# Reordering the triangular inverses of a two-block transformer kernel: one half of the heads a step ahead in the first level, two starts moved to levels four and five, and one wait on VectorE dropped

## The chip, the cores and the metric

The kernel runs on one core of one Trainium2 chip. The metric is the device time of one execution in microseconds (us). Three runs of the kernel before gave 1217.25, 1214.26 and 1218.85 us; their median is 1217.25 us.

The engines are named as in the profile: PE is the matrix engine (TensorE), PEld its weight loads, DVE the vector engine, ACT the scalar engine, POOL GpSimd, and SP the engine that issues the loads of the weights.

## What is computed

The reference runs two blocks on 256 tokens of width 1024. The first has two kinds of attention, cross attention to a memory, and a feed-forward part. The second has one layer with a recurrence over the tokens (RWKV-7) and one with latent attention, each with a feed-forward part. All of it is in 32 bits. The change lies in the recurrence, of which this is the core:

```python
def step(state, inp):
    r_t, w_t, k_t, v_t, a_t, b_t = inp
    sa = jnp.einsum('bhvk,bhk->bhv', state, a_t)
    state = (state * w_t[:, :, None, :] + sa[..., None] * b_t[:, :, None, :]
             + v_t[..., None] * k_t[:, :, None, :])
    return state, jnp.einsum('bhvk,bhk->bhv', state, r_t)
...
y = rwkv7_scan(rh, heads(decay, RWKV_HEADS), kh, vh, -kk, kk * lrh)
y = head_group_norm(y, a_lnx_g[i], a_lnx_b[i])
y = y + jnp.sum(rh * kh * a_r_k[i], axis=-1, keepdims=True) * vh
```

There are 12 heads of 64 channels. The sum over `rh * kh * a_r_k` in the last line, one number for each head and token, is what the change calls the head sums.

## The kernel before, in words

**The large products.** Most of the time goes to products of activations with weights. Weights come from HBM in units of 1 MB into a ring of four (`sync_program`). ACT makes a rounded part `w_hi` of each unit (line 2169), DVE the rest `w_lo` (line 1405, or in quarters on line 1413), and PE multiplies in three passes (line 650, the helper through which nearly all matmuls go). During the recurrence PE uses none of the streamed weights; the ring is full and the loads stand still.

**The recurrence in chunks.** The 256 tokens are cut into four chunks of 64. In a chunk the step by step update becomes products of 64x64 blocks, and needs for each head the inverse of a 64x64 triangular matrix. The 48 inverses (4 chunks of 12 heads) are computed in four batches: batch n holds the chunks 2*(n // 2) and 2*(n // 2) + 1, one on either half of the partitions, and the six heads from 6 * (n % 2) on. Batches 0 and 1 come first, then 2 and 3. The even batches use the buffers of side q = 0 (`step_142`, `inverse_140`, PSUM banks 0 and 1), the odd ones those of q = 1 (`step_143`, `inverse_141`, banks 2 and 3).

**From the products to the first inverse.** For two heads at a time PE makes the chunk products (16 instructions for the two heads in the trace, `a_and_r` and `b_and_k`) into four PSUM banks that go around. DVE masks each head's bank into SBUF (`masked`, line 2037), and PE waits for the head four places back before it writes a bank again. `first_inverse` (lines 2051 and 2054) builds the inverse to the first order, `1 + A`, for a batch, and `turn` (line 2059) transposes it. The head sums are three matmuls of 512 columns into banks 0 to 2 (`r_k` and `same_head`), before the products of heads 6 and 7; ACT copies them out (line 2569), and PE waits for these copies before it writes banks 0 to 3 for the inverses. DVE waits for the three matmuls too, in `first_inverse(0)` on line 2046.

**The levels.** Five levels double the size of the blocks that are inverted. In a level, each batch goes through a chain between two engines: "first" on PE (the chunk products times the inverse so far, 24 instructions in the trace), "first" on DVE (the mask, line 2078, tile `step`), "second" on PE (24 instructions), and "second" on DVE (the addition to `inverse_t`, line 2084, then `turn`). The `turn` feeds the "first" of the next level. After the fifth level of batch n, `turn(n + 2)` starts batch n + 2 in the same buffers, and needs `first_inverse(n + 2)`.

**The order.** `recurrence_order` gives a list of pieces, and PE, DVE and ACT each run the pieces of this one list that concern them, in its order; an engine never runs ahead of the piece that it waits for. In between lie pieces of other work: "rows" (the centred values, matmuls with `centring`), "keys" (transposes of the keys, line 1294), "high" and "low" (the parts of the next weights on ACT and DVE), "rest" (on DVE, lines 2093 and 2098), and behind the fifth level the solution itself ("rhs", "u", "state", "y"). The list of before begins so:

```python
    for level in range(1, LEVELS + 1):
        order += [("first", 0, level), ("first", 1, level)]
        order += [("rows", 2 * level - 4, 0)] if 2 <= level < 4 else []
        order += [("high", level - 1, 0)] if level <= 4 else []
        order += [("keys", level - 2, 0)] if 2 <= level < NC + 1 else [("batch", 2, 0)] if level == 1 else []
        order += [("second", 0, level), ("second", 1, level)]
        order += [("rows", 2 * level - 3, 0)] if 2 <= level < 4 else []
        order += [("batch", 3, 0)] if level == 1 else [("rest", level - 2, 0)] if level < 4 else []
```

"batch" is `first_inverse` and concerns DVE alone. Ahead of the list DVE masks the heads, makes and turns the first inverses of batches 0 and 1, and then does four operations of a token shift (`shift_pair(5, ...)`, line 1925), which the first "rows" needs.

Of the kernel before, what the change touches and what calls it, by code (L numbers as in the profile page):

```python
# [11 lines left out]
ALU = mybir.AluOpType  # L12
# [19 lines left out]
C = 64  # L32
NC = S // C
LEVELS = 5
# [571 lines left out]
def recurrence_order():  # L606


    order = []
    for level in range(1, LEVELS + 1):  # L610
        order += [("first", 0, level), ("first", 1, level)]
        order += [("rows", 2 * level - 4, 0)] if 2 <= level < 4 else []
        order += [("high", level - 1, 0)] if level <= 4 else []
        order += [("keys", level - 2, 0)] if 2 <= level < NC + 1 else [("batch", 2, 0)] if level == 1 else []
        order += [("second", 0, level), ("second", 1, level)]
        order += [("rows", 2 * level - 3, 0)] if 2 <= level < 4 else []
        order += [("batch", 3, 0)] if level == 1 else [("rest", level - 2, 0)] if level < 4 else []
# [546 lines left out]
def recurrence_tensor(k, matmul, heads_turned, attention, way_part, projection):  # L1164
    nc, PE, bank, ident = k.nc, k.nc.tensor, k.bank, k.ident[:, :]
# [70 lines left out]
    for h in range(0, RW_HEADS, 2):  # L1236
        if h in (0, 6):
            PE.wait_ge(*k.dve_once.at("r", h // 6))
        if h == 6:
            PE.wait_ge(*k.dve_once.at("rk", 0))  # L1240
            PE.wait_ge(*k.raw_made.all("ain"))
            for n in range(3):
                matmul(bank[n][:, :].rearrange("p (k t) -> p k t", k=2), k.same_head[:, :], k.rk[:, 2 * n:2 * n + 2, :], True,
                       True).then_inc(k.pe_once.sem, 1)
# [12 lines left out]
    for piece, n, level in recurrence_order():  # L1257
        if piece == "first":
            q, m, h0 = n % 2, n // 2, 6 * (n % 2)
            at = LEVELS * m + level - 1  # L1260
# [639 lines left out]
def recurrence_vector(k, attention, product, low_part, split):  # L1900
# [131 lines left out]
    def side_columns(n):  # L2032
        return k.masks[:, n:n + 1, :].to_broadcast((P, 6, C))
# [7 lines left out]
    def first_inverse(n):  # L2041
# [3 lines left out]
        if n == 0:  # L2045
            V.wait_ge(*k.pe_once.all("rk"))
# [14 lines left out]

    V.wait_ge(*k.dve_once.all("r"))
    for half in range(2):
        for h in range(6 * half, 6 * half + 6):
            masked(h)
        first_inverse(half)
        V.wait_ge(*k.xt0.at("batch", half))
        turn(half)
    shift_pair(5, 0)
    shift_pair(5, 1)  # L2070
    rest = k.rest
    for piece, n, level in recurrence_order():
        if piece == "batch":
            first_inverse(n)
        elif piece == "first":
            q, at = n % 2, LEVELS * (n // 2) + level - 1
            V.wait_ge(*k.w_p.at(f"q{q}", at))
            V.tensor_tensor(k.w[q][:, :, :], bank[2 * q][:, 0:6 * C].rearrange("p (h t) -> p h t", h=6), side_columns(2 + level),
                            ALU.mult).then_inc(k.w_v.of(f"q{q}"), 1)
# [832 lines left out]
```

## Time and profile before

| what | value |
|---|---|
| median of three runs | 1217.25 us |
| the profiled execution, its own time | 1218.09 us |
| its span in the trace | 1216.8 us |
| granted TensorE clock, mean | 0.975 |
| PE busy | 1167.8 us (96%) |
| PEld busy | 1107.5 us (91%) |
| DVE busy | 755.1 us (62%) |
| ACT busy | 572.2 us (47%) |
| POOL busy | 68.0 us (6%) |

Every time of the trace is counted from the start of the span. The profiled execution's own time is 1.3 us above its span, and 0.84 us above the median. PEclk is the share of full speed that the throttle granted to PE: 1.00 is 2.4 GHz, 0.50 is 1.2 GHz. The recurrence with its inverses lies between 588 and 686 us; the five levels of batches 0 and 1 end at 632.9 us.

### The profile page before, as it was taken

What the parts mean: (1) busy time and instruction counts of PE and PEld (TensorE: products, weight loads), DVE (VectorE), ACT (ScalarE), POOL (GpSimd) and SP (SyncE); (2) the same over time, 40 slices, a digit from 0 to 9 for tenths busy, and PEclk for the clock granted to TensorE, in tenths of its full rate; (3) what the DMA queues carried; (4) which work ended last, traced back from release to release, by engine and by line L of the source; (5) the groups of instructions that cost most, each with busy time, mean ns of one, the idle gap of its engine ahead of it and who ended that gap; (6) DMA issues with size and microseconds to landing.
All of it is one profiled execution on the core that took longest, in us unless ns stands there. A gap on an engine that the chain in (4) does not pass through costs nothing.

```text
span 1216.8 us, 22608 instructions
## 1 busy us (share of the span) xinstructions
PE 1167.8 (96%) x9917; PEld 1107.5 (91%) x9917; DVE 755.1 (62%) x982; ACT 572.2 (47%) x761; POOL 68.0 (6%) x137
## 2 busy tenths in 40 slices
PE   7998999999999999899799999999999999999998
PEld 7897978879999999889688999999987779999998
DVE  4565766556565556757786676555576776655553
ACT  5445555245444334574342545434365664543443
POOL 2310020100000000300000000000001000000000
PEclk9997999999999999998899999999999999999999
DMA  7941343424555555522000355554544205545551
GB/s 257 335 167 69 139 173 140 173 104 144 186 191 176 194 185 177 197 104 107 33 3 3 98 191 177 181 200 174 186 163 170 105 4 194 184 175 194 187 176 67
DMA packets 30237, 185.03 MB, mean 152 GB/s; under 512 B 3579, under 2 KB 6848, under 8 KB 9148
## 3 DMA queue, kind: packets, MB, share of 16 engines
q1 hardware_dynamic: 24464, 174.07, 40.0%
q0 software_dynamic: 2464, 7.11, 1.9%
q10 hardware_dynamic: 3212, 2.42, 0.6%
q8 instruction: 78, 1.28, 0.4%
q14 instruction: 19, 0.16, 0.0%
HBM read 180.18 MB, written 3.41 MB: 151 GB/s over the span
## 4 chain that ended last, share of the span: by engine, by line
PE 83%; DVE 7%; ACT 5%; issue 2%; DMA 2%; POOL 0%; SPq 0%; ACTq 0%; DVEq 0%
PE bank L650 80%; ACT w_hi L2169 2%; DMA w_raw<-in_weights 2%; DVE w_lo L1405 1%; PE bank L829 1%; ACT exps L2270 1%; DVE stats L1596 1%; PE bank L664 1%; DVE inverse_rms_rows L1531 1%; DVE logits L1588 1%; ACT x_channels_hi L2231 1%; DVE inverse L2059 0%; DVE mem_channels_gained L1440 0%; DVE inverse_t L2084 0%; ACT mem_squares L2175 0%
## 5 line engine op out<-in xcount | busy, mean ns | idle before, releaser
L1405 DVE TENSOR_TENSOR w_lo<-w_raw,w_hi 128x2048 fp32r<-128x2048 f32 x160 | 364.6, 2291 | 217.5 <-ACT w_hi L2169 217.3
L2169 ACT ACTIVATE w_hi<-w_raw 128x2048 fp32r<-128x2048 f32 x164 | 311.9, 1913 | 115.8 <-DMA w_raw<-in_weights 110.2
L650 PE MATMUL bank<-x_channels_hi,w_hi 128*128 128x256 f32 x1424 | 234.3, 288 | 10.5 <-DVE w_lo L1405 4.2
L650 PE MATMUL bank<-x_channels_lo,w_hi 128*128 128x256 f32 x1424 | 230.4, 285 | 0.0
L650 PE MATMUL bank<-x_channels_hi,w_lo 128*128 128x256 f32 x1424 | 222.8, 280 | 0.0
L650 PEld LDWEIGHTS bank<-x_channels_hi,w_hi 128*128 128x128 f32 x1424 | 198.8, 194 | 15.5 <-issue 6.9
L650 PEld LDWEIGHTS bank<-x_channels_lo,w_hi 128*128 128x128 f32 x1424 | 196.3, 192 | 0.0
L650 PEld LDWEIGHTS bank<-x_channels_hi,w_lo 128*128 128x128 f32 x1424 | 193.4, 191 | 0.0
L650 PE MATMUL bank<-hidden_hi,w_lo 128*128 128x256 f32 x528 | 103.4, 284 | 0.0
L650 PE MATMUL bank<-hidden_hi,w_hi 128*128 128x256 f32 x528 | 102.0, 280 | 0.0
L650 PE MATMUL bank<-hidden_lo,w_hi 128*128 128x256 f32 x528 | 101.7, 279 | 0.0
L650 PEld LDWEIGHTS bank<-hidden_lo,w_hi 128*128 128x128 f32 x528 | 79.8, 188 | 0.0
L650 PEld LDWEIGHTS bank<-hidden_hi,w_hi 128*128 128x128 f32 x528 | 79.3, 188 | 0.5 <-issue 0.5
L650 PEld LDWEIGHTS bank<-hidden_hi,w_lo 128*128 128x128 f32 x528 | 79.5, 188 | 0.0
L2415 ACT ACTIVATE gates<-gates 128x512 f32<-128x512 f32 x33 | 20.9, 633 | 91.2 <-DVE gates L1762 91.1
L2419 ACT ACTIVATE hidden_hi<-values 128x512 fp32r<-128x512 f32 x33 | 20.9, 632 | 89.2 <-DVE values L1769 89.2
L2270 ACT ACTIVATE exps<-logits,stats 128x128 f32<-128x128 f32 (+1 forms) x56 | 25.1, 448 | 52.6 <-DVE stats L1596 52.1
L1764 DVE TENSOR_TENSOR values<-bank,inverse_rms_rows 128x512 f32<-128x512 f32 x33 | 22.8, 690 | 37.9 <-PE bank L650 37.9
L1771 DVE TENSOR_TENSOR hidden_lo<-values,hidden_hi 128x512 fp32r<-128x512 f32 x33 | 22.9, 693 | 23.1 <-ACT hidden_hi L2419 23.1
L2231 ACT ACTIVATE x_channels_hi<-x,gain_columns 128x256 fp32r<-128x256 f32 x40 | 17.6, 501 | 38.0 <-DVE x L1503 38.0
L1762 DVE TENSOR_TENSOR gates<-bank,inverse_rms_rows 128x512 f32<-128x512 f32 x33 | 22.6, 685 | 20.7 <-ACT inverse_rms_rows L2250 20.7
L2666 POOL TENSOR_SCALAR channel_inverse_rms<-channel_mean_squares 128x2 f32<-128x2 f32 x5 | 1.2, 232 | 569.4 <-DVE channel_mean_squares L1537 569.4
(429 smaller groups left out, 1608.4 us busy)
## 6 DMA issues: line engine op xcount, KB each, us to landing
w_raw<-in_weights SPq DMA_DIRECT2D x164, 1024.0 KB, 4.8
bias_rows<-bias_lines POOLq DMA_DIRECT2D x3, 768.0 KB, 4.7
mem_rows<-in_mem POOLq DMA_DIRECT2D x2, 1024.0 KB, 5.6
bias<-bias_rows ACTq DMA_DIRECT2D x1, 1536.0 KB, 13.7
xn<-in_x SPq DMA_DIRECT2D x1, 1024.0 KB, 4.9
out<-xn SPq DMA_DIRECT2D x4, 256.0 KB, 2.2
wide_masks<-in_triangle_masks POOLq DMA_DIRECT2D x1, 832.0 KB, 6.8
bias<-bias_rows ACTq DMA_DIRECT2D x1, 768.0 KB, 5.0
```

What stands on the lines that cost most here:

```text
L650: return nc.tensor.matmul(out, lhs, rhs, start=start, stop=stop)
L664: t = nc.tensor.transpose(b[:, j * P:(j + 1) * P], k.turn_source(stage, tok, k0 + j), ident)
L829: m = nc.tensor.transpose(b[:, c:c + P], e[:, c:c + P], ident)
L1405: V.tensor_tensor(k.w_lo[:, s, :], k.w_raw[:, s, :], k.w_hi[:, s, :].bitcast(F32), ALU.subtract).then_inc(k.lo_done, 1)
L1762: V.tensor_tensor(k.gates[:, par, :, :], pairs(2 * par), R, ALU.mult).then_inc(k.gate_scaled.sem, 1)
L1764: V.tensor_tensor(k.values[:, par, :, :], pairs(2 * par + 1), R, ALU.mult).then_inc(k.up_scaled.sem, 1)
L1771: V.tensor_tensor(k.HL[:, par, :, :], k.values[:, par, :, :], k.HH[:, par, :, :].bitcast(F32), ALU.subtract).then_inc(k.hid_lo.sem, 1)
L2169: A.activation(k.w_hi[:, s, :], k.w_raw[:, s, :], ACT.Copy).then_inc(k.hi_done, 1)
L2231: A.activation(high[:, b, :], k.x[:, b, :], ACT.Copy, scale=k.split_gain(stage, part, b)).then_inc(k.x_hi.sem, 1)
L2270: e = A.activation(E[:, off[tok]:off[tok] + spans[tok]], L[:, off[tok]:off[tok] + spans[tok]], ACT.Exp, bias=stat[:, tok:tok + 1], scale=1 ...
L2415: A.activation(k.gates[:, par, :, :], k.gates[:, par, :, :], ACT.Silu).then_inc(k.silu.sem, 1)
L2419: A.activation(k.HH[:, par, :, :], k.values[:, par, :, :], ACT.Copy).then_inc(k.hid_hi.sem, 1)
```

## The change

It touches the order of the recurrence, and the places on PE and DVE that go with it:

- In level one the pieces of batch 0 run ahead: its "second" comes before the "first" of batch 1, and its "first" of level two comes before the "second" of batch 1. On DVE the mask of its first step even comes before `first_inverse(1)`. A helper `step` holds the mask that stood in the loop.
- The token shift moves from before the list to the piece "shift" behind that "first" of level two.
- `first_inverse(2)` moves from level one to the end of level four, `first_inverse(3)` from the end of level one to level five, ahead of the "second" pieces there.
- The matmuls of the head sums move from before heads 6 and 7 to before heads 10 and 11, and DVE's wait for them in `first_inverse(0)` goes. PE's wait for ACT's copies of them stays, and keeps banks 0 to 2 safe.

```diff
 def recurrence_order():
     order = []
-    for level in range(1, LEVELS + 1):
-        order += [("first", 0, level), ("first", 1, level)]
-        order += [("rows", 2 * level - 4, 0)] if 2 <= level < 4 else []
+    order += [("first", 0, 1), ("second", 0, 1), ("high", 0, 0), ("first", 1, 1), ("first", 0, 2), ("shift", 0, 0), ("second", 1, 1)]
+    for level in range(2, LEVELS + 1):
+        order += ([("first", 0, level)] if level > 2 else []) + [("first", 1, level)]
+        order += [("rows", 2 * level - 4, 0)] if level < 4 else []
         order += [("high", level - 1, 0)] if level <= 4 else []
-        order += [("keys", level - 2, 0)] if 2 <= level < NC + 1 else [("batch", 2, 0)] if level == 1 else []
+        order += [("keys", level - 2, 0)] if level < NC + 1 else []
+        order += [("batch", 3, 0)] if level == LEVELS else []
         order += [("second", 0, level), ("second", 1, level)]
-        order += [("rows", 2 * level - 3, 0)] if 2 <= level < 4 else []
-        order += [("batch", 3, 0)] if level == 1 else [("rest", level - 2, 0)] if level < 4 else []
+        order += [("rows", 2 * level - 3, 0), ("rest", level - 2, 0)] if level < 4 else [("batch", 2, 0)] if level == 4 else []
...
     for h in range(0, RW_HEADS, 2):
...
-        if h == 6:
+        if h == 10:
             PE.wait_ge(*k.dve_once.at("rk", 0))
...
         V.wait_ge(*k.g_v.at("heads", h0 + 5))
-        if n == 0:
-            V.wait_ge(*k.pe_once.all("rk"))
...
     for half in range(2):
         for h in range(6 * half, 6 * half + 6):
             masked(h)
+        if half:
+            step(0, 1)
         first_inverse(half)
         V.wait_ge(*k.xt0.at("batch", half))
         turn(half)
-    shift_pair(5, 0)
-    shift_pair(5, 1)
```

**PE, from the end of the attention to the first step.** The rows are runs of like matmuls (`r_k` with `same_head` are the head sums; `inverse_140` with `chunk_products_133` is the "first" of batch 0). Before:

```order
L650 MATMUL bank<-mem_v_102,weights_t 128x64 x8
L650 MATMUL bank<-a_and_r,b_and_k 128x128 x24
L650 MATMUL bank<-r_k,same_head 128x512 x3
L650 MATMUL bank<-a_and_r,b_and_k 128x128 x24
L650 MATMUL bank<-inverse_140,chunk_products_133 64x64 x12
L650 MATMUL bank<-inverse_141,chunk_products_134 64x64 x6
```

Now:

```order
L652 MATMUL bank<-mem_v_102,weights_t 128x64 x8
L652 MATMUL bank<-a_and_r,b_and_k 128x128 x40
L652 MATMUL bank<-r_k,same_head 128x512 x3
L652 MATMUL bank<-a_and_r,b_and_k 128x128 x8
L652 MATMUL bank<-inverse_140,chunk_products_133 64x64 x12
L652 MATMUL bank<-inverse_t,step_142 64x64 x12
```

The head sums stand behind the products of ten heads instead of six, and the "second" of batch 0 (`inverse_t,step_142`) stands ahead of the "first" of batch 1.

**DVE, from the last turn ahead of the list to the end of level one.** `step_142` and `step_143` are the masks of "first" for batches 0 and 1, `inverse_t<-bank,inverse_t` the addition of "second", `shifted` the token shift, `chunk_products_133` with `chunk_masks` the start of `first_inverse(2)`. Before:

```order
L2059 STREAM_TRANSPOSE inverse_141<-inverse_t 128x384 [waits inverse_t_first]
L1925 SCALAR_TENSOR_TENSOR shifted<-gain,cols,shifted 128x255 [waits tokens_kept,raw_channels] x4
L2078 TENSOR_TENSOR step_142<-bank,chunk_masks 128x384 [waits steps_made_0]
L2078 TENSOR_TENSOR step_143<-bank,chunk_masks 128x384 [waits steps_made_1]
L2051 TENSOR_TENSOR inverse_t<-chunk_products_133,chunk_masks 64x384 [waits chunk_products_masked]
L2051 TENSOR_TENSOR inverse_t<-chunk_products_133,chunk_masks 64x384
L2054 TENSOR_TENSOR inverse_t<-inverse_t,unit 128x384 [waits dve_steps]
L2084 TENSOR_TENSOR inverse_t<-bank,inverse_t 128x384 [waits inverse_ts_made_0]
L2059 STREAM_TRANSPOSE inverse_140<-inverse_t 128x384 [waits inverse_ts_added_0]
L2084 TENSOR_TENSOR inverse_t<-bank,inverse_t 128x384 [waits inverse_ts_made_1]
L2059 STREAM_TRANSPOSE inverse_141<-inverse_t 128x384 [waits inverse_ts_added_1]
```

Now:

```order
L2059 STREAM_TRANSPOSE inverse_141<-inverse_t 128x384 [waits inverse_t_first]
L2092 TENSOR_TENSOR inverse_t<-bank,inverse_t 128x384 [waits inverse_ts_made_0]
L2059 STREAM_TRANSPOSE inverse_140<-inverse_t 128x384 [waits inverse_ts_added_0]
L2066 TENSOR_TENSOR step_143<-bank,chunk_masks 128x384 [waits steps_made_1]
L2066 TENSOR_TENSOR step_142<-bank,chunk_masks 128x384 [waits steps_made_0]
L1927 SCALAR_TENSOR_TENSOR shifted<-gain,cols,shifted 128x255 [waits tokens_kept,raw_channels] x4
L2092 TENSOR_TENSOR inverse_t<-bank,inverse_t 128x384 [waits inverse_ts_made_1]
L2059 STREAM_TRANSPOSE inverse_141<-inverse_t 128x384 [waits inverse_ts_added_1]
L2066 TENSOR_TENSOR step_143<-bank,chunk_masks 128x384 [waits steps_made_1]
```

The mask of batch 0 (`step_142` of level one) now stands eight rows further up, ahead of `first_inverse(1)`; the addition and the turn of batch 0 follow the turn of batch 1 directly, the mask of its second level stands ahead of the shift, and `first_inverse(2)` is gone from here. `first_inverse(3)`, which followed the last of the rows of before, is gone too.

**DVE, from the last turn of level four to the second additions of level five.** Before:

```order
L2059 STREAM_TRANSPOSE inverse_141<-inverse_t 128x384 [waits inverse_ts_added_1]
L2078 TENSOR_TENSOR step_142<-bank,chunk_masks 128x384 [waits steps_made_0]
L2078 TENSOR_TENSOR step_143<-bank,chunk_masks 128x384 [waits steps_made_1]
L2084 TENSOR_TENSOR inverse_t<-bank,inverse_t 128x384 [waits inverse_ts_made_0]
L2059 STREAM_TRANSPOSE inverse_140<-inverse_t 128x384 [waits inverse_t_first]
L2084 TENSOR_TENSOR inverse_t<-bank,inverse_t 128x384 [waits inverse_ts_made_1]
```

Now:

```order
L2059 STREAM_TRANSPOSE inverse_141<-inverse_t 128x384 [waits inverse_ts_added_1]
L2051 TENSOR_TENSOR inverse_t<-chunk_products_133,chunk_masks 64x384 [waits chunk_products_masked]
L2051 TENSOR_TENSOR inverse_t<-chunk_products_133,chunk_masks 64x384
L2054 TENSOR_TENSOR inverse_t<-inverse_t,unit 128x384 [waits dve_steps]
L2066 TENSOR_TENSOR step_142<-bank,chunk_masks 128x384 [waits steps_made_0]
L2066 TENSOR_TENSOR step_143<-bank,chunk_masks 128x384 [waits steps_made_1]
L2051 TENSOR_TENSOR inverse_t<-chunk_products_134,chunk_masks 64x192 [waits chunk_products_masked]
L2051 TENSOR_TENSOR inverse_t<-chunk_products_135,chunk_masks 64x192
L2051 TENSOR_TENSOR inverse_t<-chunk_products_134,chunk_masks 64x192
L2051 TENSOR_TENSOR inverse_t<-chunk_products_135,chunk_masks 64x192
L2054 TENSOR_TENSOR inverse_t<-inverse_t,unit 128x384 [waits dve_steps]
L2092 TENSOR_TENSOR inverse_t<-bank,inverse_t 128x384 [waits inverse_ts_made_0]
```

Three operations now stand between the last turn of level four and the first mask of level five, and five between the second mask and the addition of batch 0.

## Rows read from the trace of the kernel before

**Rows 1.** The page: its first line, and the chain that ended last by engine.
```profile
span 1216.8 us, 22608 instructions
...
PE 83%; DVE 7%; ACT 5%; issue 2%; DMA 2%; POOL 0%; SPq 0%; ACTq 0%; DVEq 0%
```

**Rows 2.** Timeline of DVE, 588 to 612 us (start, duration, instructions, idle before and releaser).
```profile
593.66 1.29 DVE L2037 TENSOR_TENSOR chunk_products<-bank,chunk_masks 128x512 f32<-128x512 f32 x2 [0.37 <-PE bank L650]
596.50 1.14 DVE L2051 TENSOR_TENSOR inverse_t<-chunk_products,chunk_masks 64x384 f32<-64x384 f32 x2 [1.56 <-PE bank L650]
...
598.27 0.58 DVE L2059 STREAM_TRANSPOSE inverse<-inverse_t 128x384 f32<-128x384 f32 x1
598.77 3.79 DVE L2037 TENSOR_TENSOR chunk_products<-bank,chunk_masks 128x512 f32<-128x512 f32 x6
...
605.00 1.62 DVE L1925 SCALAR_TENSOR_TENSOR shifted<-gain,cols,shifted 128x255 f32<-128x255 f32 x4
...
607.59 1.14 DVE L2051 TENSOR_TENSOR inverse_t<-chunk_products,chunk_masks 64x384 f32<-64x384 f32 x2
...
609.24 0.55 DVE L2084 TENSOR_TENSOR inverse_t<-bank,inverse_t 128x384 f32<-128x384 f32 x1
...
610.88 0.58 DVE L2059 STREAM_TRANSPOSE inverse<-inverse_t 128x384 f32<-128x384 f32 x1
```

**Rows 3.** Timeline of PE, 588 to 606 us.
```profile
593.55 2.84 PE L650 MATMUL bank<-r_k,same_head 128*128 128x512 f32 x6
596.33 2.06 PE L650 MATMUL bank<-a_and_r,b_and_k 64*128 64x128 f32 x32
600.08 1.16 PE L650 MATMUL bank<-a_and_r,b_and_k 64*128 64x128 f32 x16 [1.69 <-DVE chunk_products L2037]
```

**Rows 4.** Stretches: length, busy of PE, PEld, DVE, ACT, POOL, then PEclk, DMA share, GB/s.
```profile
594.95:611.46 16.51, 10.09 (x172) 8.18 (x170) 14.51 (x29) 5.75 (x10) 0.00 (x0) 0.90 0.00 1
611.46:623.13 11.67, 11.38 (x228) 10.26 (x228) 9.63 (x20) 8.27 (x12) 0.00 (x0) 1.00 0.01 3
...
632.93:660.60 27.67, 27.56 (x676) 25.65 (x676) 20.73 (x38) 6.62 (x12) 0.00 (x0) 1.00 0.01 4
```

**Rows 5.** Timeline of PE, 606 to 620 us.
```profile
607.15 2.82 PE L650 MATMUL bank<-inverse_t,step 64*64 64x64 f32 x48 [1.10 <-DVE step L2078]
610.46 1.97 PE L650 MATMUL bank<-inverse,chunk_products 64*64 64x64 f32 x48 [0.49 <-DVE inverse L2059]
...
614.10 1.61 PE L650 MATMUL bank<-inverse_t,step 64*64 64x64 f32 x48
```

**Rows 6.** Timeline of DVE, 611 to 620 us.
```profile
611.49 1.28 DVE L2051 TENSOR_TENSOR inverse_t<-chunk_products,chunk_masks 64x192 f32<-64x192 f32 x4
...
613.28 1.01 DVE L2078 TENSOR_TENSOR step<-bank,chunk_masks 128x384 f32<-128x384 f32 x2
615.07 0.56 DVE L2084 TENSOR_TENSOR inverse_t<-bank,inverse_t 128x384 f32<-128x384 f32 x1 [0.77 <-PE bank L650]
```

**Rows 7.** Timeline of DVE, 626 to 640 us.
```profile
628.61 0.58 DVE L2059 STREAM_TRANSPOSE inverse<-inverse_t 128x384 f32<-128x384 f32 x1
629.15 0.56 DVE L2078 TENSOR_TENSOR step<-bank,chunk_masks 128x384 f32<-128x384 f32 x1
630.21 0.56 DVE L2078 TENSOR_TENSOR step<-bank,chunk_masks 128x384 f32<-128x384 f32 x1 [0.50 <-PE bank L650]
630.90 0.56 DVE L2084 TENSOR_TENSOR inverse_t<-bank,inverse_t 128x384 f32<-128x384 f32 x1
```

**Rows 8.** Stretches of 3.41 us before and in the second fall of the clock.
```profile
603.54:606.95 3.41, 0.92 (x24) 0.78 (x24) 3.34 (x9) 0.00 (x0) 0.00 (x0) 1.00 0.00 0
606.95:610.36 3.41, 2.82 (x48) 2.63 (x48) 3.28 (x8) 0.00 (x0) 0.00 (x0) 0.51 0.02 5
```

**Rows 9.** Stretches, PE alone (length, PE busy, PEclk, DMA share, GB/s): first fall.
```profile
579.60:583.05 3.45, 1.96 (x15) 1.00 0.33 138
...
589.87:593.30 3.43, 3.43 (x34) 0.50 0.02 5
```

More of the change, by code:

```diff
@@ L2060, in turn, with step @@
                     k.xt[:, m, h0:h0 + 6, :].rearrange("p h t -> p (h t)")).then_inc(k.x_v.of(f"q{q}"), 1)
+    def step(n, level):
+        q, at = n % 2, LEVELS * (n // 2) + level - 1
+        V.wait_ge(*k.w_p.at(f"q{q}", at))
+        V.tensor_tensor(k.w[q][:, :, :], bank[2 * q][:, 0:6 * C].rearrange("p (h t) -> p h t", h=6), side_columns(2 + level),
+                        ALU.mult).then_inc(k.w_v.of(f"q{q}"), 1)
     V.wait_ge(*k.dve_once.all("r"))
@@ L2075, in recurrence_vector @@
         elif piece == "first":
[L2076 to L2079, printed above, removed]
+            if (n, level) != (0, 1):
+                step(n, level)
+        elif piece == "shift":
+            shift_pair(5, 0)
+            shift_pair(5, 1)
         elif piece == "second":
```

## The prediction

> **What bounds the kernel.** I began with the page: by its chain PE is the last to end for 83% of the span and DVE for 7% [rows 1]. The change lies in a stretch where that is different, so I went from the page to the timelines of DVE and PE there. On DVE, from the last mask of batch 0's heads (593.66 + 1.29 = 594.95 us) to the last turn of level one (610.88 + 0.58 = 611.46 us), there is one wait, 1.56 us before 596.50, and then no more [rows 2]: the following starts come where their forerunners end, while PE is busy for only 10.09 of the same 16.51 us [rows 4]. So level one is bound by **DVE's queue**. From 611.46 to 623.13 it is the other way round: PE is busy for 11.38 of 11.67 us, DVE for 9.63 [rows 4]. Levels two and three are bound by **PE's queue**. In level five the two hand over to one another, and from 632.93, where it ends, to 660.60 PE is busy for 27.56 of 27.67 us with DVE at 20.73 [rows 4]. What counts is therefore when PE can begin that dense stretch: a delay there stays to the end, and so does a gain.
>
> **The wait of 1.56 us goes.** DVE waits at 596.50 for the head sums, whose six instructions PE ran from 593.55 to 596.39 [rows 2, 3]. With the heads masked at 594.95, DVE can go on at once: a gain of 596.50 - 594.95 = 1.55 us. What is late next is the last pair of heads. It now stands behind the head sums. PE does heads 6 and 7 from 593.6 on; heads 8 and 9 wait for the mask that ends at 594.95, and take some 1.1 us as the last pair does at 600.08 [rows 3], to 596.05; the head sums take 2.84, to 598.9; the last pair ends at 600.0. On DVE the first inverse and the turn of batch 0 take 598.77 - 596.50 = 2.27 us from 594.97, to 597.24, and four masks at 3.79 / 6 = 0.63 us each end at 599.8 [rows 2]. So DVE waits for the last pair by 0.2 us or less; I take 0.1.
>
> **Batch 2 leaves level one.** Its first inverse held DVE from 607.59 to 609.24, 1.65 us, where it had no slack [rows 2]. Gain 1.65 us. The PE work beside it ran at half clock [rows 5], and that cost nothing, since DVE did not wait for it; I count no gain for it either.
>
> **The new order in level one.** The mask of batch 0's second level comes in, 0.50 us (two of them take 1.01) [rows 6]. It has a new wait in front: batch 0's turn takes 0.58 us [rows 2] and the 24 instructions of PE behind it 0.9 (48 of them, with a 0.1 gap for a turn, take 1.97) [rows 5]; with 0.1 for the two handovers that is 1.6 us after the start of the turn, and DVE has only the turn's 0.50 and one mask of 0.50 to do in it. A wait of 0.6 us. The token shift keeps its 1.5 us (605.00 to the mask behind it) [rows 2] and only changes places; it covers the "second" of batch 1 on PE, so that costs nothing. ACT's copies of the head sums, 2 us later, have slack: PE needs them at 600.0, and the last is done some 0.6 us after 598.9. Level one together: 1.55 - 0.1 + 1.65 - 0.50 - 0.6 = **2.0 us earlier**, the last turn at 609.5 instead of 611.46.
>
> **Batch 3 leaves the end of level one.** Its five operations hold DVE from 611.49 to 613.28, 1.79 us, and then DVE still waits 0.77 us for PE [rows 6], because PE goes from the "first" of batch 1 through "rows" and "keys" to the "second" of 614.10 without it [rows 5]. It was hidden, and taking it out gains nothing. Levels two to four have the same pieces as before and only move.
>
> **Both come back in levels four and five.** There DVE goes from the turn at 628.61 straight to the mask at 629.15, waits 0.50 us before the next and 0.13 before the addition at 630.90 [rows 7]. These 0.63 us are all the cover there is. Batch 2 puts 1.65 us ahead of the first mask and batch 3 puts 1.79 us ahead of the addition, for which the turn that starts batch 2, and behind it PE's whole dense stretch, wait. PE's list has nothing between the "second" and the next "first" in level five. Cost 1.65 + 1.79 - 0.63 = **2.8 us later**.
>
> **Sum.** -2.0 + 2.8 = +0.8 us. The profiled execution took 1218.09 us with a span of 1216.8 [rows 1], so the changed kernel would take 1218.9 in such an execution; it lay 0.84 us above the median of the runs, against which I forecast 1217.25 + 0.8 = **1218.1 us**. Bounds from both sides: the gain is at most 1.55 + 1.65 = 3.2 us, if the new mask and its wait fall under something, and at least 0.9 if the last pair comes late (below). The loss is at most 1.65 + 1.79 = 3.4, with no cover at all, and at least 2.2, if both DVE waits of level five cover it and another 0.6 us of handovers does. That gives -1.0 to +2.5 us. I take the middle terms, since each is nearest to its own row.
>
> **The clock.** In the 3.41 us to 606.95 PE was busy for 0.92 us at a granted clock of 1.00; in the next 3.41 us the clock was 0.51, that is 1.2 GHz, and 48 instructions of the inverses took 2.82 us against 1.61 at 2.4 GHz [rows 5, 8]. It fell as well after a stretch with 1.96 us busy of 3.45 [rows 9]. In level five PE will now stand idle for 2.8 us more. At 2.82 against 1.61 us, 3.41 us at the low clock do the work of 1.95 us: a fall there costs 1.5 us of PE-bound time. The Trainium skill ("TensorE: Matmul & The Clock Gate", section "HAM oscillation — how this bites in real kernels") says that waits between bursts of matmuls bring the engine back to its lower clock, so that the next burst begins slowly. It speaks against this change; by that rule the result is the second case below rather than the first, and both falls in the trace agree with it.
>
> **The cases.**
> - **As summed, 1218.1 us, chance 0.5.** For it: every term is a row. Against it: handovers of 0.05 us that I could not see one by one.
> - **The clock falls once behind level five, 1217.25 + 0.8 + 1.5 = 1219.6 us, chance 0.22.** For it: the two falls. Against it: PE was busy for 10.09 of 16.51 us in level one and lost the clock once only [rows 4].
> - **The cost in levels four and five is hidden, the gain stays: 1217.25 - 2.0 = 1215.2 us, chance 0.13.** The mechanism would be that the solution behind level five waits for something else than the inverses. For it: DVE is idle for 6.9 of 27.67 us there. Against it: PE is not idle there [rows 4], and its list is in order.
> - **The wait does not go, it moves: 1219.2 us, chance 0.08.** If the clock is at half when the head sums run, they take up to twice 2.84 us, the last pair of heads comes over 1 us later, and DVE waits for it; the gain of level one shrinks to 0.9 us, the sum is +1.9. In the trace the clock rose at 593.3, just ahead of the head sums (it was 0.50 to 593.30) [rows 9]. A rise one such stretch later would do it.
> - **Slower, 1222.5 us, chance 0.07.** The place is the start of the dense stretch behind level five. If the clock falls in the idle time of level five and stays low as it did from 583.05 to 593.30, three stretches of which the last had PE busy in full [rows 9], the price is three times 1.5, and the sum 0.8 + 4.4 = +5.2 us. [...]
>
> **The numbers.** A measurement of this kernel can tell about 0.5%, 6.1 us, from no change, and all cases but corners of the last lie within that of 1217.25. To be faster by over 0.5% the kernel would have to win more than the whole wait and both first inverses together, 1.55 + 1.65 + 1.79 = 5.0 us; I leave 0.02 for what I don't see. Slower by over 0.5%: 0.04. No change: 0.94. The range takes the first four cases and the spread of the runs, 3.0 us below and 1.6 above the median: 1214.6 to 1221.4 us.
>
> **What would show it.** In the profile of the changed kernel: no wait on DVE before the first inverse of batch 0; the last turn of level one some 2 us earlier after the last mask of batch 0's heads (14.5 instead of 16.5 us); a wait of about 0.6 us before the second mask of batch 0; levels two to four of unchanged length; and in level five two waits of PE, before the "second" of batch 0 and before the "first" of batch 2, together 2.8 us longer than now, with 6.5 us instead of 632.93 - 629.19 = 3.7 from the last turn of level four to the dense stretch. I am wrong if PE does not wait there, if DVE waits for the last pair of heads by more than 0.5 us, or if PE's clock falls anywhere else in the recurrence than it did.

## The result and the profile after

The changed kernel took 1220.88 us in the median of 12 runs (1215.59 to 1223.95), the kernel before 1216.00 us (1214.26 to 1218.85, 12 runs). The ratio of their times is 1.0036, with a 95% interval of 1.0021 to 1.0051: slower by 4.4 us, between 2.6 and 6.2. The same kernel once more, on another occasion, gave 1.0023 (1.0008 to 1.0037). The forecast was 1218.1 us, 0.8 us over the kernel before, in a range of 1214.6 to 1221.4. The time lies in that range, 0.5 us from its end, but both measured intervals (2.6 to 6.2 us here, 1.0 to 4.5 in the repeat) lie above the 0.8 us. A ratio below is always the time of a run over that of the kernel before, run beside it.

The page of the changed kernel, span and chain, against [rows 1]:

```profile
span 1218.4 us, 22608 instructions
...
PE 83%; DVE 7%; ACT 5%; issue 2%; DMA 2%; POOL 0%; SPq 0%; ACTq 0%; DVEq 0%
```

The stretches that answer to [rows 4], cut at the same events: from the last mask of batch 0's heads to the last turn of level one; from there to the last turn of level two; from the last turn of level four to the first matmul of batch 2; from there to the first product of the output. Columns: length, busy of PE, PEld, DVE, ACT, POOL, then PEclk, DMA share, GB/s.

The changed kernel:

```profile
593.34:608.86 15.52, 10.89 (x158) 8.47 (x158) 13.51 (x27) 5.98 (x10) 0.00 (x0) 0.78 0.00 1
608.86:616.17 7.31, 7.17 (x114) 6.56 (x114) 2.72 (x6) 3.67 (x5) 0.00 (x0) 0.77 0.01 2
628.05:633.66 5.61, 2.53 (x73) 2.26 (x73) 5.42 (x13) 0.00 (x0) 0.00 (x0) 1.00 0.01 3
633.66:679.90 46.24, 45.65 (x999) 41.67 (x999) 34.43 (x63) 13.63 (x25) 0.00 (x0) 1.00 0.01 3
```

The kernel before, where the first of the four is the first line of [rows 4]:

```profile
611.46:617.30 5.84, 5.69 (x114) 5.13 (x114) 4.91 (x13) 3.67 (x5) 0.00 (x0) 1.00 0.01 3
629.19:632.00 2.81, 2.49 (x72) 2.26 (x72) 2.17 (x5) 0.00 (x0) 0.00 (x0) 1.00 0.03 6
632.00:678.24 46.24, 45.65 (x998) 41.67 (x999) 34.44 (x63) 13.62 (x25) 0.00 (x0) 1.00 0.01 3
```

In the kernel before the four are 16.51, 5.84, 2.81 and 46.24 us, with PEclk 0.90, 1.00, 1.00 and 1.00; levels three and four have the same length in both (5.8 and 6.06 us). So level one is 0.99 us shorter, level two 1.47 longer, the step from level four to batch 2 2.80 longer: **+3.28 us**. The profiled spans differ by only 1.6 us, since this execution of the changed kernel came to the first of these events 1.6 us earlier (593.34 against 594.95), over the same work ahead of it.

**Level one on DVE**, timeline, against [rows 2]:

```profile
592.05 1.29 DVE L2039 TENSOR_TENSOR chunk_products<-bank,chunk_masks 128x512 f32<-128x512 f32 x2 [0.36 <-PE bank L652]
593.37 1.14 DVE L2051 TENSOR_TENSOR inverse_t<-chunk_products,chunk_masks 64x384 f32<-64x384 f32 x2
...
598.45 1.29 DVE L2039 TENSOR_TENSOR chunk_products<-bank,chunk_masks 128x512 f32<-128x512 f32 x2 [0.36 <-PE bank L652]
...
604.37 0.56 DVE L2066 TENSOR_TENSOR step<-bank,chunk_masks 128x384 f32<-128x384 f32 x1 [0.59 <-PE bank L652]
605.65 0.56 DVE L2066 TENSOR_TENSOR step<-bank,chunk_masks 128x384 f32<-128x384 f32 x1 [0.72 <-PE bank L652]
...
608.28 0.58 DVE L2059 STREAM_TRANSPOSE inverse<-inverse_t 128x384 f32<-128x384 f32 x1
```

The wait of 1.56 us is gone: the mask ends at 593.34 and the first inverse starts at 593.37. Instead there are three waits: 0.36 us for the last pair of heads (0.1 was forecast), 0.59 us before the mask of batch 1 (none), and 0.72 us before the mask of batch 0's second level (0.6). The reason for the last two stands on **PE**, against [rows 5]:

```profile
600.26 0.92 PE L652 MATMUL bank<-inverse_t,step 64*64 64x64 f32 x24 [0.99 <-DVE step L2066]
602.77 2.83 PE L652 MATMUL bank<-inverse,chunk_products 64*64 64x64 f32 x48 [1.60 <-DVE inverse L2059]
605.39 1.49 PE L652 MATMUL bank<-inverse_t,step 64*64 64x64 f32 x24
608.91 1.55 PE L652 MATMUL bank<-inverse,chunk_products 64*64 64x64 f32 x24 [2.03 <-DVE inverse L2059]
```

The 48 instructions from 602.77 took 2.83 us where 1.97 was usual, the 24 from 608.91 took 1.55 instead of 0.9, and the stretches against [rows 8] show why:

```profile
598.50:602.00 3.50, 1.68 (x48) 1.40 (x46) 3.40 (x8) 3.50 (x6) 0.00 (x0) 0.99 0.00 0
602.00:605.40 3.40, 2.63 (x50) 2.63 (x51) 2.26 (x5) 0.15 (x1) 0.00 (x0) 0.50 0.02 5
605.40:608.80 3.40, 1.48 (x28) 1.29 (x26) 3.12 (x7) 0.00 (x0) 0.00 (x0) 0.50 0.00 0
608.80:612.20 3.40, 3.29 (x32) 3.17 (x33) 0.62 (x2) 0.00 (x0) 0.00 (x0) 0.50 0.00 0
612.20:615.60 3.40, 3.40 (x74) 3.05 (x74) 1.59 (x4) 3.10 (x4) 0.00 (x0) 1.00 0.02 5
```

The clock fell at 602.0, inside the wait of 1.60 us and 1.7 us after the one of 0.99; the wait of 2.03 us came while it was low. It stayed at 0.50, 1.2 GHz, for 10.2 us, to 612.2, instead of for 3.4 us. In the kernel before the low stretch lay beside a DVE that did not wait, and cost nothing. Here its first 6.9 us lie in level one, where DVE now waits for PE, and its last 3.3 us in level two, where PE is the bound.

**Level five**, DVE and then PE, against [rows 7]:

```profile
627.47 0.58 DVE L2059 STREAM_TRANSPOSE inverse<-inverse_t 128x384 f32<-128x384 f32 x1
628.08 1.14 DVE L2051 TENSOR_TENSOR inverse_t<-chunk_products,chunk_masks 64x384 f32<-64x384 f32 x2
...
629.73 1.01 DVE L2066 TENSOR_TENSOR step<-bank,chunk_masks 128x384 f32<-128x384 f32 x2
630.77 1.28 DVE L2051 TENSOR_TENSOR inverse_t<-chunk_products,chunk_masks 64x192 f32<-64x192 f32 x4
```

```profile
630.34 1.61 PE L652 MATMUL bank<-inverse_t,step 64*64 64x64 f32 x48 [1.31 <-DVE step L2066]
633.66 0.56 PE L652 MATMUL bank<-inverse,chunk_products 64*64 64x64 f32 x11 [1.71 <-DVE inverse L2059]
```

PE in the kernel before, at the second of these places (at the first, 629.99, it did not wait):

```profile
632.00 1.67 PE L650 MATMUL bank<-inverse,chunk_products 64*64 64x64 f32 x42 [0.27 <-DVE inverse L2059]
```

Nothing covers the first inverses (628.08 and 630.77): PE waits 1.31 us before the "second" of batch 0 and 1.71 before the "first" of batch 2, together 2.75 us more than before.

### The profile page after: what moved, and what is told of

Its sections match the earlier page's. It is cut to its first block, busy times and chain, and to the rows that moved or that the text cites. A ratio compares the mean times of both kernels' runs of the same rounds, so it can differ in the third digit from the quotient of the medians.

```text
span 1218.4 us, 22608 instructions
## 1 busy us (share of the span) xinstructions
PE 1168.1 (96%) x9917; PEld 1107.6 (91%) x9917; DVE 755.0 (62%) x982; ACT 572.2 (47%) x761; POOL 68.6 (6%) x137
## 3 DMA queue, kind: packets, MB, share of 16 engines
HBM read 180.18 MB, written 3.41 MB: 151 GB/s over the span
## 4 chain that ended last, share of the span: by engine, by line
PE 83%; DVE 7%; ACT 5%; issue 2%; DMA 2%; POOL 0%; SPq 0%; ACTq 0%; DVEq 0%
PE bank L652 80%; DMA w_raw<-in_weights 2%; ACT w_hi L2177 2%; DVE w_lo L1407 1%; PE bank L831 1%; ACT exps L2278 1%; PE bank L666 1%; DVE stats L1598 1%; DVE inverse_rms_rows L1533 1%; DVE logits L1590 1%; ACT x_channels_hi L2239 1%; DVE mem_channels_gained L1442 0%; DVE inverse L2059 0%; ACT mem_squares L2183 0%; DVE inverse_t L2092 0%
## 5 line engine op out<-in xcount | busy, mean ns | idle before, releaser
L1766 DVE TENSOR_TENSOR values<-bank,inverse_rms_rows 128x512 f32<-128x512 f32 x33 | 22.8, 690 | 40.3 <-PE bank L652 40.3
```

The lines of the kernel that those rows point to most:

```text
L1766: V.tensor_tensor(k.values[:, par, :, :], pairs(2 * par + 1), R, ALU.mult).then_inc(k.up_scaled.sem, 1)
```

## The experiments

Two theories went in. **A, the clock:** level five costs 2.8 us, and a longer fall of PE's clock in levels one and two takes back the gain made there. **B:** level five is all of the loss, the rest scatter. The fillers below are transposes of the identity into a PSUM bank that nobody reads at that time; they change no result.

**Fillers in level one of the changed kernel (filled).** Behind PE's "first" of batch 0, and behind its "second" of batches 0 and 1, in level one:

```diff
+    def idle_fill(n, b):
+        for _ in range(n):
+            nc.tensor.transpose(bank[b][:, 0:P], ident, ident)
...
             mm.then_inc(k.w_p.of(f"q{q}"), 1)
+            idle_fill({(0, 1): 8}.get((n, level), 0), 3)
...
             mm.then_inc(k.xt_p.of(f"q{q}"), 1)
+            idle_fill({(0, 1): 12, (1, 1): 16}.get((n, level), 0), 3 if (n, level) == (0, 1) else 7)
```

> The changed kernel with 36 transposes of the identity into unread PSUM banks, 8 behind the first matmuls of batch 0, 12 behind its second ones and 16 behind those of batch 1 in level one, where PE waits. Theory A (the clock): PE's waits in level one now lie together, the clock falls there for 10.2 us, and that costs 1.0 us in level one and 1.5 us in level two. The fillers keep PE busy, so the clock stays at 1.00 from 599 to 616 us, the stretch from the last mask of batch 0's heads to the last turn of level two shrinks from 22.8 to about 20.4 us, and the time is 2.4 us under the changed kernel, still 0.8 us above the kernel before by level five. Theory B (level five alone, the rest scatter): the fillers change the clock or not, but the time stays within 0.5 us of the changed kernel's.

Measured: 1219.49 us, ratio 1.0019 (1.0005 to 1.0033). The same four stretches:

```profile
591.72:606.39 14.67, 13.68 (x195) 10.68 (x194) 13.47 (x28) 5.98 (x10) 0.00 (x0) 1.00 0.00 1
606.39:612.22 5.83, 5.69 (x114) 5.13 (x114) 2.71 (x6) 3.66 (x5) 0.00 (x0) 1.00 0.01 3
624.11:629.72 5.61, 2.53 (x73) 2.26 (x73) 5.42 (x14) 0.00 (x0) 0.00 (x0) 1.00 0.00 0
629.72:679.00 49.28, 48.70 (x998) 44.72 (x999) 34.53 (x63) 13.61 (x25) 0.00 (x0) 0.93 0.01 3
```

With PE busy for 13.68 of 14.67 us the clock stayed at 1.00, and levels one and two took 14.67 + 5.83 = 20.5 us instead of 22.8: theory A's number. But in this execution the clock fell elsewhere, for 6.8 us from 630.6, right behind the idle time of level five; the dense stretch took 49.28 us instead of 46.24. That is the prediction's second case, at its place, at double its price. The changed kernel had the same two waits in level five, 1.31 and 1.71 us, and its clock did not fall there. The timing does not settle A against B: the median lies 1.4 us under the changed kernel's and the ratio 2.1 us under its first one, 0.5 under that of its repeat, where A wanted 2.4 and B less than 0.5, and the interval is 3 us wide.

**Fillers in level five too (filled_twice).** The edit is against the run filled. It also makes PE wait for ACT's work on the values before it writes bank 7.

```diff
             idle_fill({(0, 1): 8}.get((n, level), 0), 3)
+            if (n, level) == (1, LEVELS):
+                PE.wait_ge(*k.act_once.all("v"))
+                idle_fill(10, 7)
...
-            idle_fill({(0, 1): 12, (1, 1): 16}.get((n, level), 0), 3 if (n, level) == (0, 1) else 7)
+            idle_fill({(0, 1): 12, (1, 1): 16, (1, LEVELS): 14}.get((n, level), 0), 3 if (n, level) == (0, 1) else 7)
```

> The changed kernel with fillers in level one (36, as in the run filled) and in level five (10 behind the first matmuls of batch 1, 14 behind its second ones). In the run filled the clock stayed up in levels one and two (14.67 and 5.83 us), and fell for 6.8 us at the end of level five, where the stretch to the first product of the output took 49.3 us instead of 46.2. Theory A (the clock): with both places filled it falls in neither. Level one is 14.7, level two 5.8, the way from level four to batch 2 5.6, and the stretch behind it 46.2 us; together 84.2 us from the last mask of batch 0's heads, 0.9 over the kernel before (83.3), so the time is 0.8 us above it, the sum of the prediction. Theory B (the fall in filled had nothing to do with the idle time of level five): the clock falls there again in spite of the fillers, and the time stays 2 to 4 us above the kernel before.

Measured: 1216.90 us, ratio 0.9998 (0.9984 to 1.0012).

```profile
594.79:609.46 14.67, 13.67 (x194) 10.69 (x194) 13.47 (x27) 5.98 (x10) 0.00 (x0) 1.00 0.00 1
609.46:615.29 5.83, 5.69 (x114) 5.13 (x114) 2.72 (x6) 3.67 (x5) 0.00 (x0) 1.00 0.01 3
627.18:632.79 5.61, 5.45 (x97) 4.84 (x97) 5.42 (x13) 0.00 (x0) 0.00 (x0) 1.00 0.01 3
632.79:679.02 46.23, 45.65 (x998) 41.66 (x999) 34.42 (x63) 13.61 (x25) 0.00 (x0) 1.00 0.01 3
```

The clock fell in neither place, and the sum from the last mask of batch 0's heads to the first product of the output is 84.23 us, 0.94 over the kernel before: the prediction's +0.8, free of the clock. In the median the kernel is 4.0 us faster than the changed one; by the ratios it is 4.6 us against the first measurement of the changed kernel and 3.0 against the repeat.

**The first inverses back in level one (starts_back).** Order of the change otherwise.

```diff
-    order += [("first", 0, 1), ("second", 0, 1), ("high", 0, 0), ("first", 1, 1), ("first", 0, 2), ("shift", 0, 0), ("second", 1, 1)]
+    order += [("first", 0, 1), ("second", 0, 1), ("high", 0, 0), ("first", 1, 1), ("first", 0, 2), ("batch", 2, 0), ("shift", 0, 0), ("second", 1, 1), ("batch", 3, 0)]
...
-        order += [("batch", 3, 0)] if level == LEVELS else []
...
-        order += [("rows", 2 * level - 3, 0), ("rest", level - 2, 0)] if level < 4 else [("batch", 2, 0)] if level == 4 else []
+        order += [("rows", 2 * level - 3, 0), ("rest", level - 2, 0)] if level < 4 else []
```

> The changed kernel with the first inverses of batches 2 and 3 back in level one (batch 2 ahead of the token shift, batch 3 at its end). Level five goes back from 5.6 to 2.8 us between the last turn of level four and the first matmul of batch 2 in every theory. Theory A (the clock matters as much): level one is 1.65 us longer and PE idles longer still in it, so the clock falls there as well, and the time is between the changed kernel's minus 1.2 and the same. Theory B (the delay in level five is all of the loss): the time falls by 1.2 us against the changed kernel and lies at 1.0 us over the kernel before or less.

Measured: 1218.92 us, ratio 1.0024 (1.0008 to 1.0039).

```profile
594.32:610.75 16.43, 9.31 (x158) 6.81 (x158) 15.13 (x30) 5.98 (x10) 0.00 (x0) 0.97 0.01 1
610.75:619.14 8.39, 8.25 (x114) 7.48 (x114) 4.43 (x12) 4.60 (x7) 0.00 (x0) 0.66 0.01 2
631.03:633.85 2.82, 2.50 (x73) 2.26 (x73) 2.18 (x5) 0.00 (x0) 0.00 (x0) 1.00 0.00 0
```

Level five is back at 2.82 us, and yet the four stretches together are only 0.8 us shorter than in the changed kernel: the clock fell for 6.8 us at 609.6, inside a wait of PE of 4.38 us, and stayed low far into level two, which took 8.39 us, 2.55 over its usual length. Theory B fails here in the trace. The timing speaks less clearly: the median is 2.0 us under the changed kernel's, more than either theory wanted, and by the ratios it is 1.5 us against the first measurement and nothing against the repeat.

**The first inverses in level two (starts_in_two).** Batch 2 behind the last "second" of level one, batch 3 ahead of the "second" pieces of level two.

```diff
-    order += [("first", 0, 1), ("second", 0, 1), ("high", 0, 0), ("first", 1, 1), ("first", 0, 2), ("shift", 0, 0), ("second", 1, 1)]
+    order += [("first", 0, 1), ("second", 0, 1), ("high", 0, 0), ("first", 1, 1), ("first", 0, 2), ("shift", 0, 0), ("second", 1, 1), ("batch", 2, 0)]
...
-        order += [("batch", 3, 0)] if level == LEVELS else []
+        order += [("batch", 3, 0)] if level == 2 else []
...
-        order += [("rows", 2 * level - 3, 0), ("rest", level - 2, 0)] if level < 4 else [("batch", 2, 0)] if level == 4 else []
+        order += [("rows", 2 * level - 3, 0), ("rest", level - 2, 0)] if level < 4 else []
```

> The changed kernel with the first inverses of batches 2 and 3 in level two, where DVE waits for PE for 4.5 us. Both theories: level five is back at 2.8 us, and level two hides the 3.4 us of DVE up to some 0.4 us. Theory A: the clock falls in level one as in the changed kernel, level one and two are as long as there plus 0 to 0.4 us, and the time is 2.4 to 2.8 us under the changed kernel, within 1 us of the kernel before. Theory B: the whole gain of level one shows, the time is 1.6 us or more under the kernel before.

Measured: 1215.77 us, ratio 1.0000 (0.9988 to 1.0012). That is within 1 us of the kernel before, as theory A expected; B wanted 1.6 us less than it.

```profile
591.50:606.70 15.20, 10.48 (x160) 7.87 (x158) 13.47 (x27) 5.98 (x10) 0.00 (x0) 0.85 0.00 1
606.70:615.08 8.38, 8.24 (x114) 7.47 (x114) 6.09 (x14) 4.60 (x7) 0.00 (x0) 0.66 0.01 2
626.97:629.78 2.81, 2.49 (x72) 2.25 (x72) 2.17 (x5) 0.00 (x0) 0.00 (x0) 1.00 0.03 6
```

The clock fell for 10.2 us, from 602.1. Levels one and two took 23.58 us against 22.83 in the changed kernel, 0.75 more, where theory A had allowed 0.4; level five is back.

**The same with the fillers of level one (filled_in_two).** The two inserted lines are those of the run filled.

> The first inverses of batches 2 and 3 in level two, with the 36 fillers of level one. Theory A: the clock stays at 1.00 through levels one and two, level one is 14.7 and level two 5.8 to 6.3 us (8.38 in the run starts_in_two), level five 2.8, and from the last mask of batch 0's heads to the first product of the output it is 79.9 to 80.2 us against 83.3 of the kernel before: 3 us faster than it, by median and trace. Theory B (level two is long because DVE has the two first inverses in it, not by the clock): level two stays at 8 us or so and the time is within 1 us of the kernel before.

Measured: 1214.25 us, ratio 0.9978 (0.9964 to 0.9992).

```profile
591.81:606.48 14.67, 13.67 (x194) 10.68 (x194) 13.47 (x27) 5.98 (x10) 0.00 (x0) 1.00 0.01 1
606.48:612.75 6.27, 5.76 (x114) 5.13 (x114) 6.01 (x14) 4.11 (x6) 0.00 (x0) 1.00 0.01 3
624.64:627.45 2.81, 2.49 (x72) 2.25 (x72) 2.17 (x5) 0.00 (x0) 0.00 (x0) 1.00 0.00 0
```

Level two falls from 8.38 to 6.27 us with the same work on DVE, so it was the clock; the remaining 0.43 us over 5.84 is what two first inverses stick out of its cover. The whole is 81.89 us against 83.29 of the kernel before. My expectation of 79.9 to 80.2 was added up wrongly: its own parts, 1.84 saved and 0.43 lost, give 81.9. This version beats both kernels.

**One part of the change alone (deferred_only).** The kernel before with its two "batch" pieces moved as in the change.

```diff
-        order += [("keys", level - 2, 0)] if 2 <= level < NC + 1 else [("batch", 2, 0)] if level == 1 else []
+        order += [("keys", level - 2, 0)] if 2 <= level < NC + 1 else []
+        order += [("batch", 3, 0)] if level == LEVELS else []
...
-        order += [("batch", 3, 0)] if level == 1 else [("rest", level - 2, 0)] if level < 4 else []
+        order += [("rest", level - 2, 0)] if 2 <= level < 4 else [("batch", 2, 0)] if level == 4 else []
```

> The kernel before with one part of the change: the first inverse of batch 2 at the end of level four, that of batch 3 in level five. Level one 1.65 us shorter (less what PE at half clock makes DVE wait: 0 to 0.9), level two the same, level five 2.8 us longer. Both theories: 1.2 to 2.1 us slower than the kernel before. If the clock should stay low for longer than 3.4 us here too, the loss of the order in level one is not needed to explain it, and it is up to 1.5 us more.

Measured: 1219.57 us, ratio 1.0026 (1.0015 to 1.0037), 3.2 us slower. DVE in level one:

```profile
605.77 1.01 DVE L2079 TENSOR_TENSOR step<-bank,chunk_masks 128x384 f32<-128x384 f32 x2
607.98 0.56 DVE L2085 TENSOR_TENSOR inverse_t<-bank,inverse_t 128x384 f32<-128x384 f32 x1 [1.19 <-PE bank L651]
```

The step from level four to batch 2 took 5.60 us. Level one was 16.25 us, not 14.9: the low clock, which in the kernel before had run beside DVE's work on batch 2, now made DVE wait 1.19 us. Together that is 2.5 us in the trace, against an expectation of 1.2 to 2.1 that had allowed DVE a wait of at most 0.9.

**The other part alone (sums_only).** The kernel before with the head sums behind ten heads and without DVE's wait for them.

```diff
-        if h == 6:
+        if h == 10:
...
-        if n == 0:
-            V.wait_ge(*k.pe_once.all("rk"))
```

> The kernel before with the head sums behind ten heads and DVE's wait for them gone, nothing else. By the prediction's term DVE gains 1.55 us less 0.1 to 0.4 for the last pair of heads: level one 15.1 to 15.4 us instead of 16.5, the time 1.2 to 1.4 us lower. If the clock falls more often with the denser start, level two is longer by 1 to 2.5 us and the gain is lost. If the wait only moves, level one stays at 16 us or more.

Measured: 1216.09 us, ratio 0.9993 (0.9978 to 1.0007): its 1.2 us is too little to be told by timing. The trace shows it:

```profile
592.08 1.14 DVE L2049 TENSOR_TENSOR inverse_t<-chunk_products,chunk_masks 64x384 f32<-64x384 f32 x2
...
597.16 1.29 DVE L2037 TENSOR_TENSOR chunk_products<-bank,chunk_masks 128x512 f32<-128x512 f32 x2 [0.36 <-PE bank L650]
```

DVE goes on without a wait, and waits 0.36 us for the last pair of heads; level one took 15.30 us, level two 5.83.

Against this run the new order can be priced as well. starts_back has the head sums of this run and both first inverses in level one too, but the pieces of batch 0 run ahead: its level one took 16.43 us against 15.30, and its low clock fell there on a PE that stood idle. So the new order costs 1.1 us, the prediction's 0.50 + 0.6, and nothing comes back for it: at full clock level two is as long as before (5.83 us in filled).

**The control (before_filled).** The kernel before with 24 fillers behind the "first" of batch 0 and 8 behind that of batch 1, in level one.

```diff
             mm.then_inc(k.w_p.of(f"q{q}"), 1)
+            idle_fill({(0, 1): 24, (1, 1): 8}.get((n, level), 0), 3)
```

> The kernel before with 24 fillers behind the first matmuls of batch 0 and 8 behind those of batch 1 in level one: a control. The clock stays at 1.00 where it fell at 607 us. Theory A says that the fall cost nothing there, since DVE was the bound and waited for nothing: level one stays at 16.5 us and the time is the same within 0.5 us. If fillers brought something by themselves (another theory), it would fall by over 1 us here too.

Measured: 1217.37 us, ratio 1.0000 (0.9987 to 1.0013).

```profile
595.11:611.62 16.51, 12.68 (x204) 10.48 (x202) 14.50 (x29) 5.75 (x10) 0.00 (x0) 1.00 0.00 1
611.62:617.46 5.84, 5.69 (x114) 5.13 (x114) 4.90 (x12) 3.67 (x5) 0.00 (x0) 1.00 0.01 3
```

The clock stayed at 1.00 and neither level became shorter. Here fillers brought nothing by themselves, and the fall that DVE's queue had covered had cost nothing.

**Fillers ahead of the recurrence as well (filled_ahead).** The kernel filled_in_two with this, at the end of the memory attention:

```diff
+        for _ in range({3: 14, 4: 4}.get(i, 0)):
+            nc.tensor.transpose(bank[4][:, 0:P], ident, ident)
```

> The kernel filled_in_two with 18 more fillers where PE waits at the end of the memory attention ahead of the recurrence (14 for the wait of 1.56 us, 4 for the one of 0.48 us). In every trace so far the clock fell behind the first of these waits, to 593 us. Theory A: it falls there by the same cause, so these fillers keep it at 1.00 through the chunk products, and the time falls by another 1.5 to 4 us, to 1210 to 1213 us. Theory B (the clock falls there for another reason, such as the small attention matmuls): the time stays at 1214.2 us within 1 us, and the clock at 0.50 from about 583 us.

Measured: 1212.46 us, ratio 0.9969 (0.9958 to 0.9980), the fastest of all; its interval overlaps that of filled_in_two.

```profile
580.00:590.00 10.00, 9.21 (x103) 8.28 (x104) 8.70 (x22) 3.69 (x10) 0.00 (x0) 1.00 0.02 7
590.00:600.00 10.00, 9.92 (x119) 7.19 (x116) 9.37 (x19) 5.98 (x10) 0.00 (x0) 1.00 0.01 2
```

The clock no longer falls there, where it had been at 0.50 from 583.1 to 593.3 in the kernel before. The expectation was wrong to say that it did so in every trace: in that of filled_in_two it was low there from 585.0 to 588.4 only.

**The changed kernel once more (changed_again).**

> The changed kernel once more, beside the same runs of the kernel before, for a second profile and a narrower interval. Theory A: 3 to 5 us over the kernel before; in the profile the two sections that depend on the clock, level one and level two, need not be 15.52 and 7.31 us again, since the fall of the clock comes where its stretches happen to lie, but level one is between 14.7 and 16 us, the sum of both above 20.5 us if the clock falls there, and 5.61 us between level four and batch 2 is the same to 0.02 us. Theory B (level five alone): 0.8 to 2 us over the kernel before.

Measured: 1219.42 us, ratio 1.0023 (1.0008 to 1.0037), 2.8 us slower.

```profile
596.24:611.76 15.52, 10.89 (x158) 8.47 (x158) 13.51 (x27) 5.98 (x10) 0.00 (x0) 0.78 0.00 1
611.76:619.08 7.32, 7.17 (x114) 6.56 (x114) 2.72 (x7) 3.67 (x5) 0.00 (x0) 0.77 0.01 2
630.96:636.56 5.60, 2.53 (x72) 2.25 (x72) 5.41 (x13) 0.00 (x0) 0.00 (x0) 1.00 0.01 3
```

Its clock fell for 10.2 us again, at 605, and the three stretches are those of the first profile to 0.01 us.

## Why the prediction was right, and where it was not

The time fell in the range, but partly by luck. The sum of +0.8 us left the clock out, and the range was wide enough, with the spread of the runs, to take in what the clock cost. The range does not follow from its own words either: the lowest of the first four cases, 1215.2 us, less the 3.0 us of spread would be 1212.2, not 1214.6. Of the three signs of being wrong that the prediction named, one came: PE's clock fell elsewhere than before, from 602.0 to 612.2 us.

- **The wait of 1.56 us goes: right.** It is gone in the changed kernel and in sums_only. The new wait for the last pair of heads was 0.36 us, not 0.1; sums_only puts the step at 1.21 us.
- **Level one 2.0 us shorter: right at full clock only.** filled and filled_twice show 14.67 against 16.51 us, 1.84 us: the terms of the prediction with 0.36 us for the last pair, and with the 0.50 us that DVE waits in filled before the mask of batch 0's second level. As measured it was 0.99 us. The step that failed is "The PE work beside it ran at half clock [rows 5], and that cost nothing, since DVE did not wait for it; I count no gain for it either." It cost nothing because batch 2's first inverse kept DVE busy beside it; with that moved, the same fall is exposed, as deferred_only shows (16.25 us). In the changed kernel the fall was also three times as long, 10.2 us. I had named the clock and looked for its cost behind level five alone.
- **Levels two to four of unchanged length: wrong for level two,** 7.31 instead of 5.84 us, all of it the clock (5.83 in filled). That batch 3 was hidden is right: without it level two is no shorter.
- **Level five 2.8 us longer: right,** 2.80 in the trace and 2.79 to 2.80 in each other kernel with the late first inverses. The prediction's 3.7 and 6.5 us ran to 632.93; to the first matmul of batch 2, at 632.00 in the kernel before, they are 2.81 and 5.61, with the same difference.
- **The sum of +0.8: right free of the clock** (filled_twice: +0.94 in the trace, ratio 0.9998). Against it stand 1.47 + 0.85 = 2.3 us of clock in the profiled execution, where 0.85 is 15.52 - 14.67.
- **The cases.** I gave half of the chance to a clock as in the kernel before, and 0.22 to one more fall of 3.4 us behind level five. What came was the mechanism of the second case with the length of the last, 10.2 us, at a place that I had excused with "PE was busy for 10.09 of 16.51 us in level one and lost the clock once only". The Trainium skill's account of waits between bursts ("TensorE: Matmul & The Clock Gate", section "HAM oscillation — how this bites in real kernels") agrees with the traces in its direction: each fall in the recurrence began inside a wait of PE or at most 1.2 us behind one, and in the five profiles with fillers in level one the clock stayed up in levels one and two, while it fell there in the seven others. The page's waits are for DMA; here they were for DVE, and ones of 0.99 and 1.60 us came before or around the fall. Idle time alone does not decide it: starts_back had the same two waits and kept its clock until a third one of 4.38 us.
- **Where the clock falls differs between executions.** In the 12 runs of the changed kernel, twice (1 - mean PEclk) times the span gives 62 us at the low clock in the mean, against 54 in the 35 runs of the kernel before that were made beside filled; within the 12, each us more goes with 0.26 us of time. 8 us by 0.26 is an estimate of 2.1 us, and with 0.9 that makes 3.0, inside the measured 2.6 to 6.2. In the repeat it was 58 us against 55, which by the same estimate gives 1.7 us where 2.8 (1.0 to 4.5) was measured. Whether the rest of the 4.4 is more than scatter stays open.

## What to carry to other kernels

Where two engines take turns, ask of every low stretch of PE's clock which queue covers it: a reorder that takes work from the other engine can uncover it, and one that gathers PE's waits can lengthen it. A piece that is put earlier gains only if the engine that needs it is the one that waits: level two was bound by PE, so the new order of level one cost 1.1 us and won nothing. Work moved out of a busy place belongs where the trace shows the engine waiting for another (level two here, with 3 us and more), not where it merely comes before its use. If PE's clock falls behind a wait that can't be removed, matmuls of no use in that wait can pay: 36 to 60 of them brought 1.4 to 4.0 us here in the medians, where the low clock lay on the path, and nothing where it did not.

## What the runs showed that was not expected

The low clock lasts differently long behind the same work. Behind the waits of some 1.56 and 0.47 us at the end of the memory attention, ahead of everything that these edits touch, it lasted 10.2 us in the kernel before, 6.8 in filled and 3.4 in sums_only, so a single execution says little about the price of one fall. Filling one idle place did not keep the clock up at the next: with level one filled, it fell behind level five, where it had not fallen in either profile of the changed kernel. That is one execution, and whether the fillers had a part in it stays open.
